# Half of a feed-forward up projection by Strassen's block products, on one core of a Trainium2 chip

## The chip, the cores and the metric

The kernel runs on one core of one Trainium2 chip. The metric is the device time of one execution in microseconds, compared by its median over several runs. The engines are named as in the profile: PE (TensorE, the matmuls), PEld (its weight loads), DVE (VectorE), ACT (ScalarE), POOL (GpSimd) and SP (SyncE, which here only issues transfers). Each works through its own list of instructions in order and waits for the others through semaphores.

## The reference

One layer of an encoder and a final norm, for a group of 512 tokens and one of 256 that share the weights; the kernel treats them as T = 768 columns. Cut to what matters:

```python
h = modulate(rmsnorm(x, norm1_g[l]), sh1, sc1)
proj = h @ w_in[l]          # attention, long convolution, gates
...
x = x + g1[:, None, :] * (merged @ w_out[l])
h = modulate(rmsnorm(x, norm2_g[l]), sh2, sc2)
x = x + g2[:, None, :] * (jnp.square(jax.nn.relu(h @ w_up[l])) @ w_down[l])
shf, scf = jnp.split(c_act @ w_ada_final + b_ada_final, 2, axis=-1)
return modulate(rmsnorm(x, final_g), shf, scf)
```

The width is 1024, the inner width 4096. `w_up` is 1024 x 4096, `w_down` 4096 x 1024. `sh1` to `g2` come from a product of a vector per group with `w_ada`.

## The kernel before

Activations lie transposed: channels on the 128 partitions, tokens along a row. A weight tile is 128 output channels by 1024 input channels, eight blocks of 128 x 128. To come near the precision of float32 with faster matmuls, every operand is split into a high part (rounded) and a low part (what is left): ACT makes the high part with a copy, DVE the low part by subtracting. A product is then three passes: high x high, high weight x low activation, low weight x high activation. The 768 tokens go through in two halves of 384 (`HALF`), so a tile is 8 blocks x 3 passes x 2 halves = 48 matmuls of 384 columns (`gemm_k`, L565).

The feed-forward part runs over four chunks of 1024 inner channels (`NCH`, loops in registers, written `Fori`). In `up(c)` PE makes eight tiles of hidden channels out of `act`; ACT takes the relu out of PSUM (L1288), DVE squares it (L1784), ACT copies the high part (L1291), DVE makes the low part (L1787). In `down(c)` PE multiplies the chunk with eight tiles of `w_down`, and DVE adds each result, times the gate, to `xT` (`residual`, L1724, three pieces). Both write into two slots of `acc_ps`, two banks each, in turn; PE may begin a tile when the reader of the one two before it is done (`acc_free`). SP loads raw tiles of 512 KB into two buffers `w_raw`, each when both parts of the tile before in it are made (`hi_done`, `lo_done`).

Two things are laid beside it. DVE computes the last 24 columns of the conditioning product ("late dots", L1771 and L1774: two reductions over 1024 elements and a small addition each) out of a ring that POOL loads: eight each in `up(0)`, `down(0)` and `down(1)`. And the last down projection is done for the 512 tokens of one group first and then for the 256 of the other (`PART_ORDER`, `group_k`, L643), so that the final norm of the first runs beside the second: residual (L1732), the sum of squares (ACT L1034, DVE L1348 and L1351), a sum over partitions on PE (L628, `norm_sum`), root and reciprocal (`norm_rstd`, L1356), a spread over the partitions on PE (L636), and the output. The scale of the final norm (`norm_scale`, L1362) is computed ahead of the last up projection. The first pair of up tiles is also done by halves (`side_k`, L650), one bank at a time.

The order of the work on each engine is the order in which the code is written; there is no scheduler. What lets an instruction start are the semaphores. The four banks `wk` of PSUM are unused in this part, but for the norms.

## Time and profile before

| | before |
|---|---|
| median of 3 runs | 1191.38 us (1187.12, 1191.38, 1192.0) |
| the profiled execution, its own time | 1186.96 us |
| its span | 1185.3 us |
| PE busy | 1152.7 us, 6618 matmuls |
| PEld busy | 1072.9 us |
| DVE busy | 682.6 us, 1136 instructions |
| ACT busy | 363.4 us, 551 instructions |
| POOL busy | 76.2 us |
| granted clock of PE, mean | 0.997 |

The span is the time from the first to the last instruction of the execution that the profiler recorded; its own time is some 1.7 us longer. Busy time is the sum of what an engine executed; matmuls overlap, so that for PE the distance from one start to the next says more than the length of one. The chain that ended last follows, back from the end, who released whom; an engine that holds a large share of it sets the time. The feed-forward part begins at about 640 us and ends with the kernel.

### The profile page before, as it was taken

What the parts mean: (1) busy time and instruction counts of PE and PEld (TensorE: products, weight loads), DVE (VectorE), ACT (ScalarE), POOL (GpSimd) and SP (SyncE); (2) the same over time, 40 slices, a digit from 0 to 9 for tenths busy, and PEclk for the clock granted to TensorE, in tenths of its full rate; (3) what the DMA queues carried; (4) which work ended last, traced back from release to release, by engine and by line L of the source; (5) the groups of instructions that cost most, each with busy time, mean ns of one, the idle gap of its engine ahead of it and who ended that gap; (6) DMA issues with size and microseconds to landing.
All of it is one profiled execution on the core that took longest, in us unless ns stands there. A gap on an engine that the chain in (4) does not pass through costs nothing.

```text
span 1185.3 us, 17412 instructions
## 1 busy us (share of the span) xinstructions
PE 1152.7 (97%) x6618; PEld 1072.9 (91%) x6618; DVE 682.6 (58%) x1136; ACT 363.4 (31%) x551; POOL 76.2 (6%) x110
## 2 busy tenths in 40 slices
PE   6899999999999999999999999999999999999997
PEld 3676678889899999999889999999999999999886
DVE  6767798878455754655546776643555343233434
ACT  5621135545611211412326331122211331122314
POOL 3001110000111110000000000000000000000000
PEclk9999999999999999999999999999999999999998
DMA  9915462231342322374213343322242121212202
GB/s 350 379 54 178 160 229 100 78 102 38 117 141 98 129 99 95 107 276 140 93 50 108 123 137 130 124 89 71 73 140 82 60 71 53 71 54 71 75 32 107
DMA packets 42849, 138.69 MB, mean 117 GB/s; under 512 B 4603, under 2 KB 10315, under 8 KB 41772
## 3 DMA queue, kind: packets, MB, share of 16 engines
q1 hardware_dynamic: 26544, 81.36, 20.2%
q0 software_dynamic: 11200, 43.78, 10.7%
q10 hardware_dynamic: 5052, 12.81, 3.2%
q8 instruction: 36, 0.59, 0.2%
q14 instruction: 17, 0.14, 0.0%
HBM read 122.20 MB, written 15.74 MB: 116 GB/s over the span
## 4 chain that ended last, share of the span: by engine, by line
PE 92%; DVE 5%; issue 1%; ACT 1%; DMA 1%; SPq 0%; DVEq 0%; ACTq 0%
PE acc_ps L565 66%; PE acc_ps L643 11%; PE wk L864 3%; PE wk L690 2%; PE wk L842 2%; PE wk L783 1%; PE wk L804 1%; DMA xT_in<-in_x_T 1%; PE wk L793 1%; PE wk L683 1%; PE acc_ps L650 1%; PE wk L756 0%; PE wk L817 0%; DVE hy_cross L1619 0%; DVE dot_out L1418 0%
## 5 line engine op out<-in xcount | busy, mean ns | idle before, releaser
L565 PE MATMUL acc_ps<-act_hilo,w_hi 128*128 128x384 f32 x2304 | 503.5, 339 | 5.1 <-DVE act_hilo L1373 3.6
L565 PEld LDWEIGHTS acc_ps<-act_hilo,w_hi 128*128 128x128 f32 x2304 | 405.1, 188 | 24.9 <-issue 22.0
L565 PE MATMUL acc_ps<-act_hilo,w_lo 128*128 128x384 f32 x1152 | 292.6, 334 | 0.0
L1327 DVE TENSOR_TENSOR w_lo<-w_raw,w_hi 128x1024 fp32r<-128x1024 f32 x102 | 124.5, 1221 | 174.9 <-ACT w_hi L1016 173.1
L565 PEld LDWEIGHTS acc_ps<-act_hilo,w_lo 128*128 128x128 f32 x1152 | 208.1, 188 | 0.0
L1016 ACT ACTIVATE w_hi<-w_raw 128x1024 fp32r<-128x1024 f32 x102 | 107.8, 1057 | 287.0 <-PE acc_ps L565 283.3
L565 PE MATMUL acc_ps<-hidden_hilo,w_hi 128*128 128x384 f32 x768 | 164.0, 334 | 0.0
L565 PEld LDWEIGHTS acc_ps<-hidden_hilo,w_hi 128*128 128x128 f32 x768 | 135.9, 188 | 0.0
L565 PE MATMUL acc_ps<-hidden_hilo,w_lo 128*128 128x384 f32 x384 | 97.5, 334 | 0.0
L1724 DVE SCALAR_TENSOR_TENSOR xT<-acc_ps,modT,xT 128x384 f32 (+2 forms) x72 | 30.4, 478 | 89.9 <-PE acc_ps L565 89.3
L565 PEld LDWEIGHTS acc_ps<-hidden_hilo,w_lo 128*128 128x128 f32 x384 | 69.3, 188 | 0.0
L1418 DVE CUSTOM_DVE_ANT_0 dot_out<-dot_ring,c_rows,vecT 128x1024 f32<-128x1024 f32 x48 | 61.5, 1281 | 0.9
L1771 DVE CUSTOM_DVE_ANT_0 dot_out<-dot_ring,c_rows 128x1024 f32<-128x1024 f32 x48 | 58.7, 1223 | 3.0 <-DVE hidden_hilo L1787 2.1
L1732 DVE SCALAR_TENSOR_TENSOR xT<-acc_ps,modT,xT 128x512 f32<-128x512 f32 (+1 forms) x32 | 19.7, 617 | 61.4 <-PE acc_ps L643 61.3
L1787 DVE TENSOR_TENSOR hidden_hilo<-n_h,hidden_hilo 128x768 f32 x32 | 30.7, 958 | 38.1 <-ACT hidden_hilo L1291 38.1
L643 PE MATMUL acc_ps<-hidden_hilo,w_down_hilo 128*128 128x512 f32 (+1 forms) x288 | 50.2, 336 | 0.0
L643 PEld LDWEIGHTS acc_ps<-hidden_hilo,w_down_hilo 128*128 128x128 f32 x288 | 44.4, 190 | 5.6
L1225 ACT ACTIVATE gates_out<-acc_ps 128x768 f32<-128x768 f32 x16 | 13.0, 812 | 117.2 <-PE acc_ps L565 117.2
L1291 ACT ACTIVATE hidden_hilo<-n_h 128x768 f32 x32 | 27.1, 847 | 64.4 <-DVE n_h L1784 64.4
L1648 DVE SCALAR_TENSOR_TENSOR hy_y<-hy_xv,vecT,hy_y 128x512 f32<-128x512 f32 (+1 forms) x16 | 17.2, 1124 | 35.0 <-POOL hy_y L537 35.0
L1583 DVE CUSTOM_DVE_ANT_0 att_s<-wk,mask,sink 128x256 f32<-128x256 f32 (+1 forms) x48 | 22.5, 524 | 22.1 <-PE wk L783 22.1
L643 PE MATMUL acc_ps<-hidden_hilo,w_hi 128*128 128x256 f32 (+1 forms) x128 | 32.0, 340 | 0.8 <-DVE hidden_hilo L1787 0.8
(212 smaller groups left out, 1279.8 us busy)
## 6 DMA issues: line engine op xcount, KB each, us to landing
w_raw<-in_w_pre SPq DMA_DIRECT2D x50, 512.0 KB, 3.3
dot_ring<-in_w_ada_cols POOLq DMA_DIRECT2D x48, 512.0 KB, 3.7
w_raw<-in_w_up SPq DMA_DIRECT2D x32, 512.0 KB, 3.3
w_raw<-in_w_down SPq DMA_DIRECT2D x32, 512.0 KB, 3.3
spec<-filt_out POOLq DMA_DIRECT2D x12, 512.0 KB, 3.1
gate_spill<-gates_out ACTq DMA_DIRECT2D x16, 384.0 KB, 2.3
hy_spec<-spec SPq DMA_DIRECT2D x12, 512.0 KB, 5.6
gates_in<-gate_spill ACTq DMA_DIRECT2D x16, 384.0 KB, 4.0
```

The costliest lines, as they stand in the source:

```text
L565: mm = pe.matmul(acc_ps[:, slot, 512 * h:512 * h + HALF], w[:, kw, :], src[:, x, k, HALF * h:HALF * h + HALF], start=(first and i == 0), s ...
L643: mm = pe.matmul(acc_ps[:, slot, half(h)], w_i[:, k, :], src[:, x, k, half(h)], start=(k == 0 and i == 0), stop=(k == KD - 1 and i == 2))
L690: mm = pe.matmul(wk[:, c + 512 * odd:c + 512 * odd + 512], tab[:, 2 * p + odd, j, P * q:P * q + P], taps[:, p, (2 * r if g else 0) + odd * ...
L842: mm = pe.matmul(o, w, v, start=(i == 0), stop=(i == len(terms) - 1))
L864: mm = pe.matmul(o, w, x, start=(i == 0), stop=(i == len(terms) - 1))
L1016: act_e.activation(whi[s][:] if to is None else to[0], raw[s][:], ACT.Copy).then_inc(hi_done, 1)
L1291: act_e.activation(hid[:, 0, bass.ds(i * 2 + s, 1), :].rearrange("p o n -> p (o n)"), hfB[:, s, :], ACT.Copy).then_inc(hid_hi, 1)
L1327: dve.tensor_tensor(lo, raw[s][:], hi, ALU.subtract).then_inc(lo_done, 1)
L1418: dve.tensor_tensor_reduce(junk[:], ring[:, i], cb[:, g], 1.0, vT[:, V_BA + mt:V_BA + mt + 1], ALU.mult, ALU.add, modT[:, mt, g:g + 1]).th ...
L1724: last = dve.scalar_tensor_tensor(row, acc_piece(s, a, b), modT[:, bass.ds(gate + m, 1), g:g + 1].rearrange("p o n -> p (o n)"), row, ALU. ...
L1771: dve.tensor_tensor_reduce(junk2[:], ring2[:, s], cb2[:, g], 1.0, 0.0, ALU.mult, ALU.add, dacc[:, g:g + 1]).then_inc(dot_done, 1)
L1787: dve.tensor_tensor(hid[:, 1, m, :].rearrange("p o n -> p (o n)"), hfB[:, s, :], hid[:, 0, m, :].rearrange("p o n -> p (o n)"), ALU.subtra ...
```

## The change

Two chunks stay as they were (`NCH` = 2), one done first and one last. Between them the other 2048 inner channels are done in four groups (`NHC`), each of two pairs of up tiles, `q` = 2 hc and 2 hc + 1, and then eight down tiles over the group's 512 inner channels.

A pair of up tiles is a 2 x 2 block product: two tiles of outputs, two halves of the input channels (`PK` = 4 blocks of 128), two halves of the tokens. Strassen's scheme (Winograd's variant) makes it out of seven products of sums of blocks. The sums of the activations (`t1` to `t4`) are made once, beside the first down projection. For each pair DVE makes four sums of weight blocks (`op_sum`), ACT and DVE split seven operands (`op_high`, `op_low`), PE computes the seven products into the four banks `wk` in turn (`product`, 12 matmuls of 384 columns each), ACT copies the first out (`first_copy`) and DVE puts the others together in seven additions (`combine_st`). Relu, square and copy of the four blocks are then ACT's (`hidden`), the low parts DVE's (`hidden_low`). The late dots of the down projections move into the second up projection and the last down projection, and `norm_scale(2)` moves behind the ninth residual of the last down projection. The diff, cut to its core:

```diff
@@ -34,7 +34,12 @@
 HW = 512
 GATE0 = HY0 + 3 * HW
 DFF = 4 * D
-NCH = DFF // D
+NCH = 2
+NHC = 4
+PK = KD // 2
+ST_READ = (0, 1, 2, 3, 5, 6, 7)
+ST_DOWN = (4, 6, 5)
+ST_ORDER = ((0, 1, 2, 3, 5, 4, 6), (0, 1, 2, 3, 4, 5, 6), (0, 2, 1, 3, 5, 4, 6))
...
+        def st_ps(q, j):
+            c = 512 * ((7 * q + j) % 4)
+            return wk[:, c:c + HALF]
+
+        def op_count(r, j):
+
+            return 7 * r + ST_ORDER[min(r, 1 + (r + 1) % 2)].index(j) + 1
+
...
+            def pair_used(q, side):
+
+                n = max(op_count(q, j) for j in ((0, 2), (5,))[side])
+                sp.wait_ge(op_hi, n)
+                sp.wait_ge(op_lo, n)
+                sp.wait_ge(st_sum, 4 * q + 4)
+
...
+            for hc in range(NHC):
+                for side in range(2):
+                    pair_used(2 * hc, side)
+                    sp.dma_start(raw[side][:], w_up[2 * KD + 4 * hc + 2 + side]).then_inc(ld_sa[side], 16)
+                for m in range(KD):
+                    if m < 4:
+                        pair_used(2 * hc + 1, m // 2)
+                    else:
+                        tiles_used(KD * hc + m - 3)
+                    sp.dma_start(quarter(m % 4), w_half[KD * hc + m]).then_inc(ld_sd[m % 4], 16)
+                for side in range(2):
+                    tiles_used(KD * hc + 6 + 2 * side)
+                    if hc < NHC - 1:
+                        sp.dma_start(raw[side][:], w_up[2 * KD + 4 * hc + 4 + side]).then_inc(ld_sa[side], 16)
+                    else:
+                        sp.dma_start(raw[side][:], w_up[KD + side]).then_inc(landed[side], 16)
+            up_weights(1, first=1)
+            down_weights(1)
             for m in range(KD):
...
+            def product(q, j):
+
+                hi, lo = st_weight(j)
+                pe.wait_ge(op_hi, op_count(q, j))
+                pe.wait_ge(op_lo, op_count(q, j))
+                if (q, j) == (0, 1):
+                    pe.wait_ge(t_hi, 4)
+                    pe.wait_ge(t_lo, 4)
+                q4, j4 = divmod(7 * q + j - 4, 7)
+                if q4 >= 0 and j4 == 0:
+                    pe.wait_ge(st_p1, q4 + 1)
+                elif q4 >= 0:
+                    pe.wait_ge(st_u, 7 * q4 + ST_READ[j4])
+                for k in range(PK):
+                    for i, (w, x) in enumerate(((hi, 0), (hi, 1), (lo, 0))):
+                        mm = pe.matmul(st_ps(q, j), w[:, k, :], st_act(j, x, k),
+                                       start=(k == 0 and i == 0), stop=(k == PK - 1 and i == 2))
+                mm.then_inc(st_mm, 1)
+
+            def st_down(hc, m):
+
+                s = m % 2
+                hi, lo = st_weight(ST_DOWN[m % 3])
+                pe.wait_ge(sd_hi, KD * hc + m + 1)
+                pe.wait_ge(sd_lo, KD * hc + m + 1)
+                if hc == 0 and m < 2:
+                    pe.wait_ge(acc_free[s], A_MLP // 2 + KD)
+                else:
+                    pe.wait_ge(sd_free, KD * hc + m - 1)
+                for n, k in enumerate((0, 1, 3, 2)):
+                    if m == 0 and k != 1:
+                        need = 8 * hc + {0: 4, 3: 7, 2: 8}[k]
+                        pe.wait_ge(h4_hi, need)
+                        pe.wait_ge(h4_lo, need)
+                    for i, (w, x) in enumerate(((hi, 0), (hi, 1), (lo, 0))):
+                        for h in range(2):
+                            mm = pe.matmul(acc_ps[:, s, 512 * h:512 * h + HALF], w[:, k, :], hid4[:, x, k, HALF * h:HALF * h + HALF],
+                                           start=(n == 0 and i == 0), stop=(n == PK - 1 and i == 2))
+                mm.then_inc(sd_ready, 1)
+
             up(0, first=1)
             down(0)
-            with pe.Fori(1, NCH - 1) as c:
-                up(c)
-                down(c)
+            for hc in range(NHC):
+                for q in (2 * hc, 2 * hc + 1):
+                    for j in range(7):
+                        product(q, j)
+                for m in range(KD):
+                    st_down(hc, m)
+            pe.wait_ge(sd_free, KD * NHC)
             up(NCH - 1)
             for u, (h, m) in enumerate(PART_ORDER):
...
+            def op_high(r, j):
+
+                if j in (0, 2):
+                    act_e.wait_ge(ld_sa[0], 16 * (r + 2))
+                elif j == 5:
+                    act_e.wait_ge(ld_sa[1], 16 * (r + 2))
+                else:
+                    act_e.wait_ge(st_sum, 4 * r + {4: 1, 1: 2, 3: 3, 6: 4}[j])
+                if r == 0:
+                    act_e.wait_ge(acc_ready, A_MLP + (15 if j < 2 else 16))
+                elif r % 2 or j < 4:
+                    act_e.wait_ge(st_mm, 7 * (r - 1) + j + 1)
+                else:
+                    act_e.wait_ge(sd_ready, KD * (r // 2 - 1) + {4: 7, 5: 6, 6: 8}[j])
+                act_e.activation(st_weight(j)[0], st_source(j), ACT.Copy).then_inc(op_hi, 1)
+
...
+            def first_copy(q):
+
+                act_e.wait_ge(st_mm, 7 * q + 1)
+                if q:
+                    act_e.wait_ge(h4_lo, 4 * (q - 1) + 3)
+                act_e.activation(c_block(2), st_ps(q, 0), ACT.Copy).then_inc(st_p1, 1)
+
+            def hidden(q, b):
+
+                n = 4 * q + b + 1
+                act_e.wait_ge(st_u, 7 * q + (2, 4, 6, 7)[b])
+                act_e.activation(c_block(b), c_block(b), ACT.Relu).then_inc(st_relu, 1)
+                act_e.wait_ge(st_relu, 2 * n - 1)
+                act_e.activation(c_block(b), c_block(b), ACT.Square).then_inc(st_relu, 1)
+                act_e.wait_ge(st_relu, 2 * n)
+                act_e.activation(hid_block(q, b, 0), c_block(b), ACT.Copy).then_inc(h4_hi, 1)
...
+            def op_low(r, j):
+
+                dve.wait_ge(op_hi, op_count(r, j))
+                hi, lo = st_weight(j)
+                dve.tensor_tensor(lo, st_source(j), hi, ALU.subtract).then_inc(op_lo, 1)
+
+            def down_low(hc, m):
+
+                dve.wait_ge(sd_hi, KD * hc + m + 1)
+                hi, lo = st_weight(ST_DOWN[m % 3])
+                dve.tensor_tensor(lo, quarter(m % 4), hi, ALU.subtract).then_inc(sd_lo, 1)
+
+            def combine_st(q, n):
+
+                j = (1, 2, 3, 4, 4, 5, 6)[n]
+                dve.wait_ge(st_mm, 7 * q + j + 1)
+                if n < 2:
+                    dve.wait_ge(st_p1, q + 1)
+                else:
+                    dve.wait_ge(st_u, 7 * q + (0, 0, 2, 3, 1, 4, 5)[n])
+                if q and n in (0, 1, 3):
+                    dve.wait_ge(h4_lo, 4 * (q - 1) + {0: 4, 1: 1, 3: 2}[n])
+                dst, other = (c_block(b) for b in ((3, 2), (0, 2), (2, 3), (1, 2), (3, 3), (2, 2), (3, 3))[n])
+                dve.tensor_tensor(dst, st_ps(q, j), other, ALU.add).then_inc(st_u, 1)
+
+            def hidden_low(q, b):
+
+                dve.wait_ge(h4_hi, 4 * q + b + 1)
+                dve.tensor_tensor(hid_block(q, b, 1), c_block(b), hid_block(q, b, 0), ALU.subtract).then_inc(h4_lo, 1)
+
+            def st_residual(hc, m):
+
+                s = m % 2
+                dve.wait_ge(sd_ready, KD * hc + m + 1)
+                if hc == 0:
+                    dve.wait_ge(acc_free[s], A_MLP // 2 + KD)
+                else:
+                    dve.wait_ge(sd_free, KD * (hc - 1) + m + 1)
+                for g, a, b in PIECES:
+                    last = dve.scalar_tensor_tensor(xT[:, m, a:b], acc_piece(s, a, b), modT[:, G2 + m, g:g + 1],
+                                                    xT[:, m, a:b], ALU.mult, ALU.add)
+                last.then_inc(sd_free, 1)
+
...
+            for hc in range(NHC):
+                q = 2 * hc
+                combine_st(q, 0)
...
+                else:
+                    op_sum(q + 1, 0)
+                    op_sum(q + 1, 1)
+                    op_low(q + 1, 0)
+                    op_low(q + 1, 1)
+                    combine_st(q, 1)
+                    op_sum(q + 1, 2)
+                    op_sum(q + 1, 3)
+                    combine_st(q, 2)
+                    hidden_low(q, 0)
+                    op_low(q + 1, 2)
+                    combine_st(q, 3)
+                    combine_st(q, 4)
+                    op_low(q + 1, 3)
+                combine_st(q, 5)
+                hidden_low(q, 1)
+                if hc == 0:
+                    op_low(1, 3)
+                op_low(q + 1, 4)
+                combine_st(q, 6)
+                hidden_low(q, 2)
+                op_low(q + 1, 5)
+                q = 2 * hc + 1
+                hidden_low(q - 1, 3)
+                op_low(q, 6)
+                combine_st(q, 0)
+                combine_st(q, 1)
+                combine_st(q, 2)
+                hidden_low(q, 0)
+                combine_st(q, 3)
+                combine_st(q, 4)
+                down_low(hc, 0)
+                combine_st(q, 5)
+                hidden_low(q, 1)
+                combine_st(q, 6)
+                hidden_low(q, 2)
+                down_low(hc, 1)
+                hidden_low(q, 3)
+                down_low(hc, 2)
+                for m in range(KD):
+                    if m == KD - 1 and hc < NHC - 1:
+                        op_sum(q + 1, 3)
+                        op_low(q + 1, 3)
+                        op_low(q + 1, 5)
+                    st_residual(hc, m)
+                    if m + 3 < KD:
+                        down_low(hc, m + 3)
+                    if m >= KD - 2 and hc == NHC - 1:
+                        split_w(T_MLP + 16 + m % 2, m % 2, 16 * (landed_base + 9))
+                    if m == 5 and hc < NHC - 1:
+                        op_low(q + 1, 0)
+                        op_low(q + 1, 2)
+                    if m == 6 and hc < NHC - 1:
+                        op_sum(q + 1, 0)
+                        op_sum(q + 1, 1)
+                        op_sum(q + 1, 2)
+                        op_low(q + 1, 1)
+                    if m == KD - 1 and hc < NHC - 1:
+                        op_low(q + 1, 4)
+                        op_low(q + 1, 6)
+            dve.wait_ge(ld_c, 48)
+            up(NCH - 1, dots=KD)
             for u, (h, m) in enumerate(PART_ORDER):
                 dve.wait_ge(acc_ready, A_MLP + 16 * (NCH - 1) + KD + u + 1)
-                dve.wait_ge(acc_free[u % 2], A_MLP // 2 - 3 + KD * (NCH - 1) + m // 2)
+                if not h:
+                    dve.wait_ge(sd_free, KD * (NHC - 1) + m + 1)
                 residual_group(u % 2, m, G2, h)
                 if u < KD - 2:
                     t = T_MLP + 16 * (NCH - 1) + KD + u + 2
                     split_w(t, u % 2, 16 * (landed_base + (t - T_MLP) // 2 + 1), to=w_last(u + 2))
                 if u <= KD or u == 2 * KD - 1:
                     acc_half(2, u, h)
+                if u < KD:
+                    late_dot(2 * KD, u // 2, u % 2)
                 if u == KD:
+                    dve.wait_ge(late_done, DOTS - DOTS_OUT + 1)
+                    norm_scale(2)
                     norm_rstd(2, 0)
```

In the odd pairs of a group no weights of a next pair are prepared; those of the group behind are prepared beside its down tiles. How the change stands on the engines, at three places.

DVE, one up tile before (the low part of a weight tile, the square, the low part of the hidden tile, registers and a wait between them):

```order
L1327 TENSOR_TENSOR w_lo1<-w_raw1,w_hi1 128x1024
L1784 TENSOR_TENSOR n_h<-ev_tmp 128x768
L1785 REGISTER_ALU
L1787 ISA
L1787 REGISTER_ALU
L1787 TENSOR_TENSOR hidden_hilo<-n_h,hidden_hilo 128x768
```

DVE, the beginning of an even pair after the change (`c_st` are the blocks being put together, `s1_sum` to `s4_sum` sums of weight blocks of the odd pair behind it, `w_lo0`, `w_lo1` low parts):

```order
L2100 TENSOR_TENSOR c_st<-wk,c_st 128x384
L2075 TENSOR_TENSOR s1_sum<-w_raw1 128x512
L2075 TENSOR_TENSOR s2_sum<-s1_sum,w_raw0 128x512
L2081 TENSOR_TENSOR w_lo0<-w_raw0,w_hi0 128x512
L2081 TENSOR_TENSOR w_lo0<-s2_sum,w_hi0 128x512
L2100 TENSOR_TENSOR c_st<-wk,c_st 128x384
L2075 TENSOR_TENSOR s3_sum<-w_raw0,w_raw1 128x512
L2075 TENSOR_TENSOR s4_sum<-w_raw0,s2_sum 128x512
L2100 TENSOR_TENSOR c_st<-wk,c_st 128x384
L2105 TENSOR_TENSOR hid_st<-c_st,hid_st 128x384
L2081 TENSOR_TENSOR w_lo1<-w_raw0,w_hi1 128x512
L2100 TENSOR_TENSOR c_st<-wk,c_st 128x384 x2
```

Where DVE had a low part, a square and a low part of 768 or 1024 elements for each tile, it now has additions out of PSUM with the sums and low parts of the next pair between them.

ACT, the end of an odd pair after the change (L1486 relu, L1488 square, L1490 high part of a hidden block; L1473 high part of a down tile of the same group):

```order
L1486 ACTIVATE c_st<-c_st 128x384
L1488 ACTIVATE c_st<-c_st 128x384
L1490 ACTIVATE hid_st<-c_st 128x384
L1473 ACTIVATE w_st_hilo<-w_raw0 128x512
L1486 ACTIVATE c_st<-c_st 128x384
L1488 ACTIVATE c_st<-c_st 128x384
L1490 ACTIVATE hid_st<-c_st 128x384
L1473 ACTIVATE w_st_hilo<-w_raw1 128x512 x2
```

The last hidden block of the group stands behind the high part of the second down tile.

DVE, the end of the first group of tokens in the last down projection, before and after (its last two residuals and what follows, L1732 and L1992 are the residual):

```order
L1732 SCALAR_TENSOR_TENSOR xT<-acc_ps,modT,xT 128x512
L1351 TENSOR_TENSOR n_acc<-n_acc,n_t 128x512
L1732 SCALAR_TENSOR_TENSOR xT<-acc_ps,modT,xT 128x256
L1348 COPY n_acc<-n_sq 128x256
L1356 RECIPROCAL norm_rstd<-norm_rstd 128x4
```

```order
L1992 SCALAR_TENSOR_TENSOR xT<-acc_ps,modT,xT 128x512
L1611 TENSOR_TENSOR n_acc<-n_acc,n_t 128x512
L2031 ISA dot_out2,dot_sum<-dot_ring2,c_rows2 128x1024
L2031 ISA dot_sum 128x1
L2031 ISA dot_out2,dot_sum<-dot_ring2,c_rows2 128x1024
L2031 ISA dot_sum 128x1
L2034 TENSOR_SCALAR modT<-dot_sum,vecT 128x2
L1992 SCALAR_TENSOR_TENSOR xT<-acc_ps,modT,xT 128x256
L1608 COPY n_acc<-n_sq 128x256
L1622 SCALAR_TENSOR_TENSOR norm_scale<-modT,vecT 128x8 x2
L1616 RECIPROCAL norm_rstd<-norm_rstd 128x4
```

A late dot stands between the eighth residual's accumulation and the ninth residual, and the norm scales stand ahead of the reciprocal.

## Rows read from the trace of the kernel before

**Rows 1.** The page: busy time by engine, and the chain that ended last
```profile
PE 1152.7 (97%) x6618; PEld 1072.9 (91%) x6618; DVE 682.6 (58%) x1136; ACT 363.4 (31%) x551; POOL 76.2 (6%) x110
...
PE 92%; DVE 5%; issue 1%; ACT 1%; DMA 1%; SPq 0%; DVEq 0%; ACTq 0%
```

**Rows 2.** The chain in order of time: start us, us, what
```profile
484.00 83.20 PE acc_ps L565 x480
...
655.16 449.58 PE acc_ps L565 x2592
```

**Rows 3.** Timeline, first up tiles: start us, us, engine line op tiles
```profile
652.64 0.51 PE L650 MATMUL acc_ps<-act_hilo,w_hi 128*128 128x384 f32 x2
```

**Rows 4.** Waits from 600 us on: total us, times, longest us
```profile
DVE hidden_hilo L1787 <- ACT hidden_hilo L1291: 38.1, 32, 1.2
...
PE acc_ps L643 <- DVE hidden_hilo L1787: 0.8, 1, 0.8
```

**Rows 5.** Groups by form, DVE and ACT: busy us, mean ns, idle before
```profile
L1327 DVE TENSOR_TENSOR w_lo<-w_raw,w_hi 128x1024 fp32r<-128x1024 f32 x58 | 70.8, 1220 | 104.8 <-ACT w_hi L1016 104.0 <-issue 0.8
...
L1388 DVE TENSOR_TENSOR act_hilo<-n_h,act_hilo 128x512 fp32r<-128x512 f32 x8 | 5.5, 684 | 1.2 <-ACT act_hilo L1067 1.2
...
L1388 DVE TENSOR_TENSOR act_hilo<-n_h,act_hilo 128x256 fp32r<-128x256 f32 x8 | 3.4, 425 | 2.4 <-ACT act_hilo L1067 2.4
...
L1067 ACT ACTIVATE act_hilo<-n_h 128x512 fp32r<-128x512 f32 x8 | 5.1, 632 | 0.3
...
L1067 ACT ACTIVATE act_hilo<-n_h 128x256 fp32r<-128x256 f32 x8 | 3.3, 418 | 0.3
```

**Rows 6.** Timeline, first matmul of a down tile, ACT, a residual
```profile
705.21 0.85 PE L565 MATMUL acc_ps<-hidden_hilo,w_hi 128*128 128x384 f32 x4
...
705.49 1.06 ACT L1016 ACTIVATE w_hi<-w_raw 128x1024 fp32r<-128x1024 f32 x1 [3.31 <-PE acc_ps L565]
...
714.50 1.27 DVE L1724 SCALAR_TENSOR_TENSOR xT<-acc_ps,modT,xT 128x384 f32 x3 [0.53 <-DVE modT L1774]
```

**Rows 7.** Timeline, DVE: one dot
```profile
716.82 1.22 DVE L1771 CUSTOM_DVE_ANT_0 dot_out<-dot_ring,c_rows 128x1024 f32<-128x1024 f32 x1
...
717.96 0.08 DVE L1771 DVE_READ_ACCUMULATOR2_ANT dot_sum<- 128x1 f32 x1
...
719.58 0.23 DVE L1774 TENSOR_SCALAR modT<-dot_sum,vecT 128x2 f32 x1 [0.27 <-DVE dot_sum L1771]
```

**Rows 8.** Timeline of the last down projection, DVE and PE
```profile
1109.27 0.96 DVE L1787 TENSOR_TENSOR hidden_hilo<-n_h,hidden_hilo 128x768 f32 x1 [1.23 <-ACT hidden_hilo L1291]
...
1110.38 0.70 PE L643 MATMUL acc_ps<-hidden_hilo,w_hi 128*128 128x512 f32 x2 [0.84 <-DVE hidden_hilo L1787]
...
1111.35 0.75 DVE L1732 SCALAR_TENSOR_TENSOR xT<-acc_ps,modT,xT 128x512 f32<-128x512 f32 x1 [1.12 <-PE acc_ps L643]
...
1116.82 0.75 DVE L1732 SCALAR_TENSOR_TENSOR xT<-acc_ps,modT,xT 128x512 f32<-128x512 f32 x1 [3.25 <-PE acc_ps L643]
...
1118.62 0.69 DVE L1351 TENSOR_TENSOR n_acc<-n_acc,n_t 128x512 f32<-128x512 f32 x1
...
1150.90 0.69 DVE L1351 TENSOR_TENSOR n_acc<-n_acc,n_t 128x512 f32<-128x512 f32 x1 [0.70 <-ACT n_t L1034]
...
1151.77 0.95 PE L628 MATMUL wk<-ones,n_acc 128*128 128x1 f32 x8
...
1153.22 0.48 DVE L1732 SCALAR_TENSOR_TENSOR xT<-acc_ps,modT,xT 128x256 f32<-128x256 f32 x1 [1.63 <-PE acc_ps L643]
...
1154.40 0.17 DVE L1356 RECIPROCAL norm_rstd<-norm_rstd 128x4 f32<-128x4 f32 x1
...
1154.62 1.16 PE L636 MATMUL wk<-ident,norm_rstd 128*128 128x128 f32 x8 [0.73 <-DVE norm_rstd L1356]
```

**Rows 9.** Norm scale by form (1038 to 1106 us); a weight load, us to landing
```profile
L1362 DVE SCALAR_TENSOR_TENSOR norm_scale<-modT,vecT 128x8 f32<-128x8 f32 x2 | 0.2, 160 | 0.0
...
w_raw<-in_w_up SPq DMA_DIRECT2D x32, 512.0 KB, 3.3
```

More of the change, by code:

```diff
@@ new lines, in t_high @@
+            def t_high(n, src, dst):
+                act_e.wait_ge(t_step, n)
+                act_e.activation(dst, src[:], ACT.Copy).then_inc(t_hi, 1)
+            up(0)
+            for u in range(KD):
+                if u < KD - 2:
+                    split_w(T_MLP + KD + 2 + u, u % 2, 16 * (landed_base + 6 + u // 2))
+                if u == 1:
+                    t_high(3, t_f1, t1[:, 0])
+                if u == 2:
+                    t_high(5, t_f2, t2[:, 0])
+                if u == 5:
+                    t_high(10, t_f2, t3[:, 0])
+                    act_e.wait_ge(t_lo, 3)
+                    t_high(10, t_f1, t4_hi[:])
@@ L1943, in laid_out @@
     h["w_up"] = tiles(np.asarray(inputs["w_up"])[0])
[L1944 to L1945 removed]
+    down = np.asarray(inputs["w_down"])[0]
+    h["w_down"] = np.concatenate([tiles(down[D * i:D * i + D]) for i in range(NCH)])
+    h["w_down_half"] = np.concatenate([tiles(w) for w in down[D * NCH:].reshape(NHC, PK * P, D)])
     return {n: np.ascontiguousarray(v) for n, v in h.items()}
```

249 lines of the change are left out of this document (211 added, 38 removed).

## The prediction

> **What bounds the kernel.** I read the page first: TensorE (PE) is busy for 97% of the span, and 92% of the chain that ended last is PE [rows 1]. The reader should see that ACT and DVE can only matter where PE waits for them. Then the chain in order of time: the feed-forward part is one piece, 2592 matmuls of 384 columns in 449.58 us, so 173.4 ns from start to start [rows 2]. Straight-line code does the same: 480 in 83.20 us, 173.3 ns. So neither the loops nor their absence cost PE anything. In the list of waits PE waits only once from there on before the end of the last down projection, 0.8 us for the last hidden tiles [rows 4]. Whatever removes matmuls there removes time, as long as PE stays fed.
>
> **What it removes.** A pair of up tiles took 2 tiles x 8 k x 3 passes x 2 token halves = 96 matmuls; seven products of 4 k x 3 passes are 84. Eight pairs: 96 matmuls fewer. The new ones write one bank in a row instead of two in turn. The first up tiles already do that: two in 0.51 us with 334 ns for one, so the second starts some 0.17 us after the first [rows 3]. Hence 96 x 173.4 ns = **16.6 us gained**. The down half keeps its number: 4 x 8 tiles x 4 k x 3 x 2 = 768 matmuls, as before. Weight bytes do not change.
>
> **What it adds on DVE and ACT.** Prices, from the lengths of like instructions [rows 5]: on DVE 1024 elements take 1220 ns, 512 take 684, 256 take 425; so 384 take 0.555 us and 1536 (the activation sums) about 1.76. On ACT 512 take 632, 256 take 418, so 384 take 0.525. Neighbours overlap by about 0.08 us (the next DVE instruction after 716.82 + 1.22 started at 717.96). PE's end is seen 0.28 us after the next tile's first matmul started (705.21 to 705.49) [rows 6]; DVE's end is seen by PE after 0.14 us (1109.27 + 0.96 to 1110.38) [rows 8].
> - *The seven sums of the activations*, with their splits (ten sums, four highs, four lows), stand in the first down projection, where each tile gives DVE 8.3 us (48 x 173.4 ns). The fullest tile, the seventh, has a residual of 1.27 us [rows 6], two lows of 1536 and four 512-long ones: 1.27 + 3.4 + 2.5 = 7.2 us. It fits with about 1 us left; price nothing. Without that cover the first product would wait by the excess.
> - *An even pair* (its products take 84 x 0.1734 = 14.6 us) also carries the split of the odd pair behind it: 11 instructions of 512 and 11 of 384 on DVE, 11 x 0.684 + 11 x 0.555 = 13.6 us, less 21 overlaps of 0.08 = 11.9 us. It starts late: in the last two tiles of the down before it, seven 512-long instructions stand between the seventh residual and the eighth, which ends 2.9 us after that tile's matmuls (-4.16 + 0.28 + 1.27 + 7 x 0.604 + 1.27); two lows follow, to 4.1. The first combine can start at 4.4 (two products of 2.08, 0.28 until seen). Combine and four 512-long: 7.3, the second combine; it and two sums: 9.1, the third; then the first hidden low waits for ACT (7.9 + three steps of 0.545 = 9.5), itself and a 512-long low bring 10.8, the fourth, and 11.3, the fifth; from there PE sets the pace, 12.8 and 14.9. The bank of the second product is wanted back at 10.4 (by the sixth), those of the third to fifth at 12.5, 14.6 and 16.6: four and a half microseconds are spare, and about four for the weights of the fifth to seventh product. The raw pairs take 3.3 us to land [rows 9] and are asked for about when the even pair starts; the first sum wants them at 4.9. Price nothing.
> - *An odd pair* has half that work. Here one wait is real. The down tile that follows takes its inner blocks in the order 0, 1, 3, 2; block 2 is read after 18 matmuls, at 3.12 us, and needs the hidden block made from the last product. That is: 0.28 until seen, combine 0.555, but ACT is still in the high part of a down tile until 1.05; relu, square and copy, each waiting for the one before, 3 x 0.545 = 1.63, to 2.7; the low part 0.555, to 3.25; 0.14 to PE, 3.4. PE waits **0.3 us, four times: 1.2 us**. No row shows such a chain; from below it is 0 (ACT 0.3 us earlier each time), from above 1.0 each, 4 us, if the three ACT steps and the two hand-offs cost a third more. I take 1.2, next to the rows.
> - *PE waits for the last residual* before the second up projection (a wait on all 32 residuals, where there were two buffers): 0.28 + 1.27 + 0.14 = **1.7 us**, once. Queued behind are the whole up projection's matmuls. Nothing hides it.
> - *The dots that were in the down projections* move: eight to the second up, eight to the last down. In the up they cost nothing (the first up carries the same eight without holding PE up). In the last down a tile of 512 columns lasts 5.44 us (5.47 for the first, 1111.35 to 1116.82). One dot is two reductions and an addition, 716.82 to 719.81, 2.91 us to the next instruction [rows 7]. Walk: hidden low ends at 1110.23, then comes the last up dot: DVE is free at 1113.4 where the first residual stood at 1111.35, 2.1 us late. A tile then needs 1.80 + 0.61 + 2.91 = 5.32 us (the accumulation starts 1.80 us after its residual, 1118.62 after 1116.82), so the lag shrinks 0.12 us a tile to 1.4 at the seventh tile; without a split the period is 4.97, the eighth residual is 0.9 us late. PE's sum for the norm at 1151.77 needs the accumulation of 1150.90 + 0.69 + 0.9 = 1152.5: **0.7 us**. Behind it stands the eighth dot, DVE is free at 1155.3, and the ninth residual (1153.22) is 2.1 us late; then the two norm scales, moved here, 2 x 160 ns less overlaps [rows 9]. The reciprocal of 1154.40 comes at 1156.75, PE's spread of 1154.62 at 1156.97: **2.35 us in all**, the 0.7 included. Bounds: 0 if DVE caught up by then, 5.4 (a tile) if each dot took half a microsecond longer.
>
> **Sum.** 16.6 - 1.2 - 1.7 - 2.35 = 11.4 us off the profiled execution: its own 1186.96 us becomes 1175.6 (the span 1185.3 becomes 1173.9). The three runs before it were 1187.12, 1191.38 and 1192.0; on their median the same gain gives **1180.0 us**, -0.96%.
>
> **A rule that speaks against it.** The fixed part of a DVE instruction here is what is left at zero length of 1220 and 684 ns: 0.15 us, half of it overlapped. The Trainium skill, page "VectorE: DVE Perf Modes", in its section on the TRN2 errata, says that VectorE and ScalarE pay a latency between instructions and advises tiles of at least 512 elements, so that it carries less weight; the change goes the other way, with 384-long pieces. By the page's formula of (N + 151)/0.96 ns, an estimate, 384 elements take 0.557 us, where the rows give 0.555; the sum stays. It feeds the chance of the next rival, nothing else.
>
> **Rivals.**
> 1. *DVE becomes the bound in the even pairs: slower than before.* It happens if the hand-offs from ACT are exposed: seven lows wait for their highs, four hidden lows for ACT's copy. Before, such a wait is 38.1 us / 32 = 1.19 us [rows 4]. All eleven exposed: 11.9 + 13.1 = 25 us, where a pair's 14.6 and the 4.5 spare allow 19.1; PE loses 5.9 us in each of four even pairs: 24 - 11.4 = 12 us slower, 1204. PE starts to wait at a DVE stretch of 19.1 us (0.65 us a hand-off), and the kernel is slower than before above 22 (0.9). For it: DVE's load is 82% of PE's, the waits exist. Against: in the order written, other DVE work stands between nearly every high and its low, and ACT has its own slack (about 11 us in 14.6).
> 2. *Small stalls eat half.* The chain behind the last product costs 1.0 instead of 0.3 (+2.8), the last down loses a whole tile (+3): gain 5.6, 1185.8. For it: three margins in the walk are under 1 us (block 2, the seventh tile of the first down, the lag in the last down). Against: each length comes from a row.
> 3. *Everything is hidden but the 1.7 us:* gain 14.9, 1176.5. It needs ACT 0.3 us earlier four times, and a DVE that catches up 2.1 us in seven tiles; the dots alone speak against it.
>
> **Chances.** Forecast 0.66; rival 1 0.07 in full, and 0.04 at the threshold of no change; rival 2 0.13; rival 3 0.10. About 0.5%, 6 us, is what a measurement of this kernel can tell. Forecast and rival 3 are faster, and a third of rival 2: 0.80. Same 0.13, slower 0.07. The range: 1173 (rival 3 on a run like the lowest, 1187.12) to 1187 (rival 2 with a run like the highest).
>
> **What would show it.** The products: 672 matmuls of 384 columns into wk, 173 ns apart, none with a wait; 2.08 us a product. In the list of waits: PE for hid_st four times, near 0.3 us; PE for the last residual once, 1.7; PE's norm sum and spread together 2.35 above before. DVE about 12 busy us per even pair. A granted clock of 1.00 through it, as now. I am wrong if PE waits in the middle of a pair, for a low part or for a bank, if the products stand further apart than 173 ns, or if the last down tiles show DVE without idle time and PE waiting for weights.

## The result and the profile after

| | changed kernel | kernel before |
|---|---|---|
| median, us (runs) | 1177.72 (4) | 1191.69 (4) |
| lowest to highest, us | 1177.17 to 1180.96 | 1187.12 to 1192.14 |
| ratio of the times | 0.9888, 95% interval 0.9867 to 0.9908 | |

The changed kernel is 1.1% faster; the forecast was 1180.0 us. The execution that was profiled is its longest, 1180.96 us, with a span of 1179.3.

The page of the changed kernel, against [rows 1]: 96 matmuls fewer, 9 us less of PE, 206 instructions and 96 us more on DVE. That PE's busy time falls by 9 us, and not by the 16.6 us of the matmuls that went, is the lower clock of this execution, 0.990 against 0.997: in *tail* and *best* below, at 0.997, it falls by 16.5 and 17.1. In the row PEclk the second place, 29 to 59 us, is now 8, ahead of the part that was changed. What the clock does behind PE's waits is too short for slices of 29 us and is shown below.

```profile
PE 1143.8 (97%) x6522; PEld 1061.9 (90%) x6522; DVE 778.9 (66%) x1342; ACT 413.6 (35%) x683; POOL 76.9 (7%) x111
...
PEclk9899999999999999999999999999999999999998
```

Its chain in order of time (start us, us, what), the counterpart of [rows 2]. L1103 is a product, 168 matmuls being an even and an odd pair; L1124 is a down projection of half the inner channels.

```profile
658.90 116.75 PE acc_ps L677 x672
775.65 29.12 PE wk L1103 x168
804.77 33.41 PE acc_ps L1124 x192
838.18 29.12 PE wk L1103 x168
867.30 33.43 PE acc_ps L1124 x192
...
992.38 33.46 PE acc_ps L1124 x192
...
1027.56 68.45 PE acc_ps L677 x384
...
1101.66 39.04 PE acc_ps L755 x171
...
1147.00 1.16 PE wk L748 x8
1148.16 20.94 PE acc_ps L755 x162
```

What to see: each pair of pairs takes 29.12 us, and the next entry starts at once. 29.12 / 168 is 173.3 ns, so no product waits. The 384 matmuls of the last up loop take 68.45 us where 384 x 173.3 is 66.57, and the last 162 take 20.94 where before they took 19.45 (same view of the kernel before, from 1155.78). The feed-forward part, from the first entry above to the end of the span, is 1179.3 - 658.90 = 520.4 us; before it is 1185.3 - 655.16 = 530.1 [rows 2]. So 9.7 us came out of the part that was changed.

PE's waits in this part (total us, times, longest us), the counterpart of [rows 4]:

```profile
PE wk L748 <- DVE norm_rstd L1616: 2.4, 2, 1.8
PE acc_ps L677 <- DVE xT L2116: 1.7, 1, 1.7
PE wk L740 <- DVE n_acc L1611: 1.5, 1, 1.5
PE acc_ps L755 <- DVE hidden_hilo L2047: 0.9, 1, 0.9
```

The third and fourth stand in the kernel before as well (1.5 and 0.8). The second is new. The first was 0.7 at its longest [rows 8].

Behind both long waits the granted clock falls. Stretches of 2 us (columns: us, then busy time of each engine, PEclk, DMA share, GB/s), first behind the wait for the last residual, then behind the wait for the norm:

```profile
1026.00:1028.00 2.00, 0.44 (x2) 0.44 (x3) 2.00 (x4) 0.00 (x0) 0.00 (x0) 1.00 0.60 246
1028.00:1030.00 2.00, 2.00 (x10) 2.00 (x10) 0.26 (x1) 0.00 (x0) 0.00 (x0) 0.69 0.34 35
1030.00:1032.00 2.00, 2.00 (x8) 2.00 (x7) 0.00 (x0) 0.00 (x0) 0.00 (x0) 0.50 0.61 227
1032.00:1034.00 2.00, 2.00 (x13) 2.00 (x12) 0.00 (x0) 0.00 (x0) 0.00 (x0) 0.95 0.00 0
...
1147.00:1149.00 2.00, 2.00 (x14) 2.00 (x15) 0.69 (x1) 0.02 (x1) 0.00 (x0) 0.81 0.00 0
1149.00:1151.00 2.00, 2.00 (x12) 2.00 (x11) 0.00 (x0) 0.79 (x1) 0.00 (x0) 0.50 0.16 60
```

PE is busy for the whole of a stretch and does only 8 matmuls in it, instead of 13: 0.50 is 1.2 GHz. The loop behind the wait of 1.7 us thus took 1.9 us more than its matmuls. Of these 1.6 are the clock's: where it holds, as in *again* below, the loop still takes 66.85 us, 0.3 more than 66.57. A busy column does not show this; the count in it and PEclk do.

DVE in the even pair that starts at 838.18 (timeline: start us, us, ...), for which the prediction had a walk:

```profile
842.38 0.56 DVE L2100 TENSOR_TENSOR c_st<-wk,c_st 128x384 f32<-128x384 f32 x1
844.97 0.69 DVE L2075 TENSOR_TENSOR s_sum<-w_raw 128x512 f32<-128x512 f32 x1 [2.04 <-DMA w_raw<-in_w_up]
...
847.75 0.55 DVE L2100 TENSOR_TENSOR c_st<-wk,c_st 128x384 f32<-128x384 f32 x1
...
851.09 1.02 DVE L2100 TENSOR_TENSOR c_st<-wk,c_st 128x384 f32<-128x384 f32 x2
```

The first, second and fourth combine start 4.2, 9.6 and 12.9 us into the pair; the walk had 4.4, 7.3 and 10.8. DVE stood for 2.04 us because the raw pair had landed only at 6.8, and not before 4.9: SP issued its two loads only from 838.78 to 840.29. PE did not notice.

The last down projection, DVE and PE (timeline), the counterpart of [rows 8]:

```profile
1104.72 0.75 DVE L1992 SCALAR_TENSOR_TENSOR xT<-acc_ps,modT,xT 128x512 f32<-128x512 f32 x1
...
1106.85 1.22 DVE L2031 CUSTOM_DVE_ANT_0 dot_out<-dot_ring,c_rows 128x1024 f32<-128x1024 f32 x1
...
1109.52 0.75 DVE L1992 SCALAR_TENSOR_TENSOR xT<-acc_ps,modT,xT 128x512 f32<-128x512 f32 x1
...
1114.58 0.74 DVE L1992 SCALAR_TENSOR_TENSOR xT<-acc_ps,modT,xT 128x512 f32<-128x512 f32 x1
...
1140.72 0.75 DVE L1992 SCALAR_TENSOR_TENSOR xT<-acc_ps,modT,xT 128x512 f32<-128x512 f32 x1 [0.62 <-PE acc_ps L755]
...
1143.04 0.95 PE L740 MATMUL wk<-ones,n_acc 128*128 128x1 f32 x8
...
1145.45 0.48 DVE L1992 SCALAR_TENSOR_TENSOR xT<-acc_ps,modT,xT 128x256 f32<-128x256 f32 x1
```

Count from the start of the down, 1101.66 here and 1110.38 before. The first residual stands at 3.06 instead of 0.97, which is 2.1 late. A late tile lasts 5.06 us on DVE (1109.52 to 1114.58) and 5.44 on PE, so the lag is gone before the eighth: its residual is at 39.06, before 39.08, and waits for PE. The norm sum is at 41.38, before 41.39. Only the last dot still stands ahead of the ninth residual: 43.79 instead of 42.84, and the spread is at 45.34 instead of 44.24, 1.1 late.

### The profile page after: what moved, and what is told of

The parts are those of the page before. It is cut to its first block, busy times and chain, and to the rows that moved or that the text cites. A ratio compares the mean times of both kernels' runs of the same rounds, so it can differ in the third digit from the quotient of the medians.

```text
span 1179.3 us, 17099 instructions
## 1 busy us (share of the span) xinstructions
PE 1143.8 (97%) x6522; PEld 1061.9 (90%) x6522; DVE 778.9 (66%) x1342; ACT 413.6 (35%) x683; POOL 76.9 (7%) x111
## 4 chain that ended last, share of the span: by engine, by line
PE 92%; DVE 4%; issue 1%; ACT 1%; DMA 1%; SPq 0%; DVEq 0%; ACTq 0%
PE acc_ps L677 44%; PE acc_ps L1124 11%; PE acc_ps L755 11%; PE wk L1103 10%; PE wk L976 3%; PE wk L802 2%; PE wk L954 2%; PE acc_ps L762 1%; PE wk L895 1%; PE wk L916 1%; PE wk L905 1%; PE wk L795 1%; DMA xT_in<-in_x_T 1%; PE wk L868 0%; PE wk L929 0%
## 5 line engine op out<-in xcount | busy, mean ns | idle before, releaser
L677 PE MATMUL acc_ps<-act_hilo,w_hi 128*128 128x384 f32 x1792 | 398.1, 343 | 6.1 <-DVE act_hilo L1633 3.0
L677 PEld LDWEIGHTS acc_ps<-act_hilo,w_hi 128*128 128x128 f32 x1792 | 317.8, 190 | 26.6 <-issue 23.5
L677 PE MATMUL acc_ps<-act_hilo,w_lo 128*128 128x384 f32 x896 | 229.2, 336 | 0.0
L677 PEld LDWEIGHTS acc_ps<-act_hilo,w_lo 128*128 128x128 f32 x896 | 163.5, 190 | 0.0
L1587 DVE TENSOR_TENSOR w_lo<-w_raw,w_hi 128x1024 fp32r<-128x1024 f32 x70 | 85.5, 1222 | 91.9 <-ACT w_hi L1172 90.9
L1124 PE MATMUL acc_ps<-hid_st,w_st_hilo 128*128 128x384 f32 x768 | 134.3, 335 | 0.0
L1124 PEld LDWEIGHTS acc_ps<-hid_st,w_st_hilo 128*128 128x128 f32 x768 | 133.0, 188 | 0.7 <-issue 0.7
L2116 DVE SCALAR_TENSOR_TENSOR xT<-acc_ps,modT,xT 128x384 f32<-128x384 f32 (+2 forms) x96 | 40.6, 479 | 58.9 <-PE acc_ps L1124 58.9
L677 PE MATMUL acc_ps<-hidden_hilo,w_hi 128*128 128x384 f32 x256 | 54.7, 334 | 0.0
L1992 DVE SCALAR_TENSOR_TENSOR xT<-acc_ps,modT,xT 128x512 f32<-128x512 f32 (+1 forms) x32 | 19.7, 616 | 39.7 <-PE acc_ps L755 39.5
L677 PEld LDWEIGHTS acc_ps<-hidden_hilo,w_hi 128*128 128x128 f32 x256 | 45.3, 188 | 0.0
L1473 ACT ACTIVATE w_st_hilo<-w_raw 128x512 fp32r<-128x512 f32 x32 | 20.2, 630 | 69.5 <-PE acc_ps L1124 62.9
```

Of the source, the lines that this page charges most:

```text
L677: mm = pe.matmul(acc_ps[:, slot, 512 * h:512 * h + HALF], w[:, kw, :], src[:, x, k, HALF * h:HALF * h + HALF], start=(first and i == 0), s ...
L1124: mm = pe.matmul(acc_ps[:, s, 512 * h:512 * h + HALF], w[:, k, :], hid4[:, x, k, HALF * h:HALF * h + HALF], start=(n == 0 and i == 0), sto ...
L1587: dve.tensor_tensor(lo, raw[s][:], hi, ALU.subtract).then_inc(lo_done, 1)
L2116: last = dve.scalar_tensor_tensor(xT[:, m, a:b], acc_piece(s, a, b), modT[:, G2 + m, g:g + 1], xT[:, m, a:b], ALU.mult, ALU.add)
```

## Experiments

My theory after this result: the matmuls removed are worth their full 16.6 us; against them stand the wait for the last residual (1.7 us and some 1.9 by the clock), the late dots (1.1 and some 1.5 by the clock) and almost nothing else. The rivals are those of the prediction, above all a DVE that is about to be the bound. The numbers below are medians, and the feed-forward part of the profiled execution (from the first matmul of its first up loop to the end of the span), since the kernel's first 60 us vary by themselves (last section). The first four kernels were timed beside each other in 5 rounds (kernel before: 1191.62 us, 11 runs), the other four in 3 rounds on another chip (1190.64, 13 runs).

**The changed kernel again** (*again*), no edit.

> The changed kernel itself, beside its variants on the same chip. Theory: all its matmuls' gain is there, 16.6 us, and it gives back 6.7: PE waits 1.7 us for the last residual and 1.8 us at the norm's spread (0.7 before), and after each of these the granted clock stands at half for about 3.4 us, which costs 1.9 and 1.5 us. From the first tile of the up loop to the end I expect 520.4 us (530.1 in the kernel before); over the runs 11 to 14 us less than before. Rival: the 13 us between the medians is mostly the start of the program and the feed-forward part gives less than 8.

Measured: 1179.68 us, ratio 0.9905 (0.9883 to 0.9928); part 520.0 us. The waits are the same, 1.7 and 1.8. The clock is not. Behind the 1.7 us wait it holds, and the last up loop takes 66.85 instead of 68.45 us. Behind the 1.8 us wait it falls earlier than in the first trace, and eight matmuls of the spread take 2.07 us instead of 1.16. Stretches of this run:

```profile
1028.00:1030.00 2.00, 2.00 (x14) 2.00 (x13) 0.00 (x0) 0.00 (x0) 0.00 (x0) 1.00 0.65 150
...
1144.00:1150.00 6.00, 5.41 (x25) 5.41 (x26) 1.22 (x5) 0.94 (x2) 0.00 (x0) 0.50 0.12 44
```

So the same wait of the same kernel is followed by a fall in one execution and not in another.

**The wait for the residuals, one slot at a time** (*slot*)**.** The second up projection starts when 31 of the 32 residuals are done, and its second tile waits for the last.

```diff
-            pe.wait_ge(sd_free, KD * NHC)
-            up(NCH - 1)
+            pe.wait_ge(sd_free, KD * NHC - 1)
+            up(NCH - 1, last=KD * NHC)
...
+                        if last is not None and s == 1:
+                            pe.wait_ge(sd_free, last)
```

> PE waits before the second up projection only for the residual of the slot that it writes: the first tile for the seventh residual of the last group, the second for the eighth. Theory (the wait brings the fall of the clock): the wait of 1.7 us goes and the 1.9 us at half clock with it, 3.6 us less than the changed kernel; clock 1.00 from 1020 to 1040 us. Rival (the fall has another cause, such as the new mix of work): 1.7 us less and still some 3.4 us at half clock near that place.

Measured: 1174.54 us, ratio 0.9857 (0.9833 to 0.988); part 515.6 us, 4.3 less than the changed kernel beside it. In its chain the loop follows the down at once and runs at full clock:

```profile
993.83 33.41 PE acc_ps L1126 x192
1027.23 66.57 PE acc_ps L677 x384
...
1145.93 19.45 PE acc_ps L755 x162
```

The 1.7 us is gone from the list of waits. Of the 4.3, 1.7 is the wait and 0.3 the loop. The clock behind the spread gives 2.8, since it held here though its wait of 1.8 us is still there, and 0.5 is lost again in the last 10 us. These two are not the edit's doing. As the clock did not fall behind the 1.7 us wait in *again* either, this pair of traces does not settle whether the wait brings the fall; *group* does.

**The late dots one place earlier** (*tail*)**.** Each dot of the last down moves a tile forward, the first of them to the head of the second up projection; none stands ahead of the ninth residual any more (the two buffers that the rows for the dots are loaded into change places with them).

```diff
+            late_dot(KD, 0, 0)
-            up(NCH - 1, dots=KD)
+            up(NCH - 1, dots=KD + 1)
...
-                if u < KD:
-                    late_dot(2 * KD, u // 2, u % 2)
+                if u < KD - 1:
+                    late_dot(2 * KD + 1, u // 2, u % 2)
```

> The sixteen moved late dots come one place earlier: one ahead of the second up projection, eight in it, seven in the last down projection, none between the eighth and the ninth residual. Theory: the ninth residual is no longer behind a dot; PE waits about 0.7 us at its norm sum and 0.7 to 0.8 at the spread, each too short for the clock to fall: 0.4 us of waits and 1.5 us of half clock less, 1.9 in all. Rival (the clock falls after any wait there, or PE's total idle counts): 0.4 us less, clock still 0.5 near 1150 us.

Measured: 1177.34 us, ratio 0.9888 (0.9864 to 0.9912), 2.3 below the changed kernel beside it, which the scatter of the medians covers; part 516.2 us, 3.7 less. The waits say it more clearly: the longest for the norm is 0.9 instead of 1.8, and the last 162 matmuls take 19.45 us.

```profile
PE wk L748 <- DVE norm_rstd L1616: 1.4, 2, 0.9
```

Of the 3.7, 2.8 is the clock, which held behind the spread. That the shorter wait is why it held is not shown: in *slot*, *eight* and *group* it held behind 1.8 us too. Here the 1.7 us wait was again without a fall of the clock (66.85 us for the loop).

**Both, and the last hidden block ahead of the second down tile's weights** (*best*)**.** On ACT and on DVE the step for the last hidden block goes one place forward, so that a wait for it in the down projection would go.

```diff
-                down_high(hc, 1)
                 hidden(q, 3)
+                down_high(hc, 1)
...
-                down_low(hc, 1)
                 hidden_low(q, 3)
+                down_low(hc, 1)
```

> Both of these, and the last hidden block of each group ahead of the second down tile on ACT and DVE. Theory: 3.6 + 1.9 + 0.5 = 6.0 us less than the changed kernel, 1.6% less than before; no half clock but in the last 10 us. Rival (no clock effect): 1.7 + 0.4 + 0.5 = 2.6 us less.

Measured: 1170.75 us, ratio 0.9838 (0.9813 to 0.9864), the fastest of all, 1.6% below the kernel before and 8.9 us below the changed one. The part is 514.3 us, 5.7 less. Of the 5.7, 2.8 is once more the clock behind the spread in *again*; the waits that are gone or shorter give the rest. The other 3.2 are the part ahead of it: three of its four runs had a mean clock of 0.997, the six of the changed kernel 0.988 to 0.994. The down projections:

```profile
800.39 33.41 PE acc_ps L1126 x192
...
1021.39 66.57 PE acc_ps L677 x384
```

192 x 173.3 is 33.28, so 0.13 us stay in each (the three not shown are 33.43, 33.41 and 33.41). The edit did not bring the block earlier. Timelines of the first of these down projections in the changed kernel and then here (first matmul, the last low part of a hidden block, the weight load behind the first 18):

```profile
804.61 3.58 PE L1124 MATMUL acc_ps<-hid_st,w_st_hilo 128*128 128x384 f32 x19
807.07 0.56 DVE L2105 TENSOR_TENSOR hid_st<-c_st,hid_st 128x384 fp32r<-128x384 f32 x1 [0.64 <-ACT hid_st L1490]
807.75 0.30 PEld L1124 LDWEIGHTS acc_ps<-hid_st,w_st_hilo 128*128 128x128 f32 x2 [0.17 <-issue]
...
800.23 3.58 PE L1126 MATMUL acc_ps<-hid_st,w_st_hilo 128*128 128x384 f32 x19
802.69 0.56 DVE L2108 TENSOR_TENSOR hid_st<-c_st,hid_st 128x384 fp32r<-128x384 f32 x1 [1.24 <-ACT hid_st L1492]
803.36 0.30 PEld L1126 LDWEIGHTS acc_ps<-hid_st,w_st_hilo 128*128 128x128 f32 x2 [0.17 <-issue]
```

In both the low part ends 3.02 us into the down projection, and PE loads the 19th weights 0.12 or 0.11 us after it, having stood for 0.17. ACT's relu for this block starts 0.79 us in, in both, so the high part of the down tile that stood ahead of it had not held it up. This is the wait that the prediction derived, at the place that it named, only shorter.

**Eight for seven** (*eight*)**.** The seventh product is computed twice: 12 matmuls more in each pair, 96 in all, and nothing else.

```diff
-                for k in range(PK):
+                for k in [k for _ in range(2 if j == 6 else 1) for k in range(PK)]:
```

> The seventh product of each pair is computed twice in a row (its first twelve matmuls are overwritten), so a pair has 96 matmuls again and everything else stays. Theory (the gain is the matmuls taken out, and PE is the bound in every pair): 8 x 12 x 173.3 ns = 16.6 us more than the changed kernel, from the first tile of the up loop to the end 536.6 to 537 us; a pair of products 16.64 us where it is 14.56. Rival (part of the gain is hidden because PE would wait for DVE or ACT in the pairs anyway): less than 12 us more, with waits of PE gone.

Measured: 1197.23 us, ratio 1.0063 (1.0041 to 1.0084), 17.5 above the changed kernel's 1179.68; part 535.4 us, 1.2 below what was expected, since the clock held behind the spread (19.45 us for the last 162 matmuls), though it fell behind the last residual (68.43 for the loop). Its chain gives the price without scatter:

```profile
773.09 33.28 PE wk L1103 x192
```

33.28 - 29.12 = 4.16 us for 24 matmuls, 16.64 for the four groups. The removed product is worth the whole of its matmul time. Without it the changed kernel is slower than the one before by what the reordering costs.

**PE waits for the last residual ahead of groups 2 to 4** (*group*)**.**

```diff
             for hc in range(NHC):
+                if hc:
+                    pe.wait_ge(sd_free, KD * hc)
```

> PE also waits, ahead of the products of groups 2 to 4, for the last residual of the group before, which DVE ends 2.9 us after the last down matmul (it stands behind seven instructions for the next pair). Theory (a wait costs itself and may bring the clock down behind it): three waits of 3.0 us, 9.0 us; and behind each the clock at half for up to 3.4 us, up to 1.7 us each, 5 more: 9 to 14 us more in that part, and a clock of 0.5 in windows behind the waits. Rival (no effect on the clock from waits of this length): 9.0 us and clock 1.00.

Measured: 1193.34 us (10 runs), ratio 1.0018 (1.0003 to 1.0033), 13.7 above the changed kernel; part 532.7 us (from 659.80), 12.7 more. The waits add up to 8.9 us:

```profile
PE wk L1103 <- DVE xT L2118: 8.9, 3, 3.0
```

They are 3.0 each, not 1.7, since other DVE work stands between the last two residuals there, as in the prediction's walk. Behind all three the clock falls; the third:

```profile
976.00:978.00 2.00, 1.21 (x4) 1.21 (x5) 1.94 (x5) 0.00 (x0) 0.00 (x0) 0.50 0.89 322
...
980.00:982.00 2.00, 2.00 (x8) 2.00 (x7) 0.00 (x0) 0.96 (x2) 0.00 (x0) 0.50 0.00 0
```

The 168 products of that group take 32.07 us instead of 29.12, 2.95 more. The 0.3 that stands behind a wait at full clock is in it, so some 2.7 are the clock's. At these three places the clock of the changed kernel is 1.00, and nothing but PE's waits was added: this is the run that shows that a wait brings the fall. Three waits of PE between the groups eat the whole gain.

**More work for DVE in the even pairs** (*lows1*, *lows2*)**.** The rival that DVE is nearly the bound: each of the seven low parts that it makes for the odd pair is computed twice (once more), then three times (twice more). One costs 0.7 us with its wait, so 5 and 10 us in each even pair.

```diff
                 hi, lo = st_weight(j)
+                for _ in range(1 if r % 2 else 0):
+                    steps[0] += 1
+                    dve.tensor_tensor(lo, st_source(j), hi, ALU.subtract).then_inc(f_step, 1)
+                    dve.wait_ge(f_step, steps[0])
```

> Each low part of an odd pair's operands is made twice, the second after the first has ended: seven instructions, 7 x 0.72 = 5.0 us more on DVE in each even pair. Theory (DVE has slack there, about 2.4 us at the tightest bank and more behind): PE waits under 0.5 us a pair, the kernel is at most 1 us longer. Rival (DVE is at its limit in the even pairs): 4 x 3 to 5 us, 12 to 20 us longer, slower than before.

Measured, once more: 1182.13 us, ratio 0.9931 (0.9905 to 0.9956), 2.5 to 4.4 above the changed kernel's two medians. PE waits 3.5 us in all for it:

```profile
PE acc_ps L1124 <- DVE hid_st L2109: 3.0, 5, 0.8
...
PE wk L1103 <- DVE c_st L2104: 0.5, 1, 0.5
```

The theory had at most 1, the rival 12 to 20. The part is 523.3 us (from 657.01), 3.3 more. The rival falls, but the slack is smaller than I had it: 5 us more are already felt at the hidden blocks.

> The same with each of these low parts made three times: 10 us more on DVE in each even pair. The bank of the third product, wanted at 12.5 us and read at 10.1 now, is read at 13.0; what follows gets later by up to 10 us, less some 3.5 us in which DVE waits now. Theory: PE waits 2 to 5 us in each even pair or at the start of the odd one, 8 to 20 us in all, and each wait may bring the clock down. Rival (the prediction's walk, 4.5 us spare and 19.1 us allowed for a stretch of 21.9): 2.8 us a pair, 11 us. Both are waits for combines, not for low parts.

Measured, twice more: 1205.8 us, ratio 1.0131 (1.0111 to 1.0152); part 544.9 us (from 659.30).

```profile
PE wk L1103 <- DVE c_st L2104: 14.2, 16, 2.7
PE acc_ps L1124 <- DVE hid_st L2109: 4.6, 8, 0.8
```

18.8 us of waits, within what was expected. So the mechanism of the rival is real: PE waits for a bank that a combine has yet to free, and the kernel ends on the slower side. The point from which it decides lies between 5 and 10 us more of DVE in an even pair.

## Why the prediction was right, step by step

1. *What it removes, 16.6 us.* Right to the digit: 29.12 us for 168, and 16.64 taken back by the eighth product. That the seven products write one bank in a row cost nothing.
2. *The seven sums in the first down projection, price nothing.* Right. 672 matmuls in 116.75 us are 0.3 above 672 x 173.3, as much as the 2592 of before were above theirs.
3. *An even pair, price nothing.* Right in the price, wrong in the walk. DVE was busy 12.6 us in the stretch 838 to 853, near the 11.9 that I had. But from the second combine on it was 2.1 to 2.3 us late, since I gave the raw pair 3.3 us to land from the start of the pair, and it landed at 6.8. That was half of the 4.5 us that I held to be spare, which fits with 5 us more for DVE being felt and 10 hurting.
4. *An odd pair, 0.3 us four times.* The down projections were 0.13 to 0.18 us above 192 x 173.3, 0.6 in all, not 1.2. The wait is at block 2, where I had it, and its size was wrong. I held ACT busy with the high part of a down tile until 1.05; it was done by 0.89, and the relu started at 0.79, right behind the combine. So the low part ended at 3.02 and not at 3.25, and PE gets there at 3.12: with the 0.14 of the hand-off it is late by hundredths, and 0.13 is the whole of what each down projection loses.
5. *The last residual, 1.7 us.* Measured 1.74, and gone when the wait was split by slots. What I priced was the wait alone; the loop behind it takes 0.3 more even at full clock (66.85 against 66.57).
6. *The last down projection, 2.35 us.* Measured 1.1. The step that failed is the length of a dot. I took 2.91 us from [rows 7], where its last addition had waited 0.27 us for the second reduction; in the last down the dots took 2.67 (1106.85 to 1109.52). A tile of DVE was then 5.06 us instead of 5.32, and the lag, which began at the 2.1 that I had, lost 0.38 a tile instead of 0.12. It was gone before the norm sum (0.7 expected, 0.0 measured), and only the eighth dot was left, with 0.95.
7. *"A granted clock of 1.00 through it, as now."* Wrong. In the profiled execution 1.9 us were lost behind the last residual, 1.6 of them by the clock and the 0.3 of step 5, and 1.5 by the clock behind the spread. The prediction had looked for what PE waits for, and put what a wait does to the clock at nothing.

The sum for this execution: -16.6 + 0.6 + 1.7 + 1.9 + 1.1 + 1.5 = -9.8 us, measured -9.7; predicted -11.4. The terms mis-sized (together 1.85 us too dear) and what was left out (3.4) partly cancel, so the time was nearer than the working deserves. That is luck, and so is some of the agreement of the medians. Between the medians it is -14.0 us in the first comparison and -11.9 in the second; the difference to the part is made ahead of it, where the code is the same in both kernels (last section).

Of the rivals, the first exists but is 5 to 10 us of DVE away from deciding. The second, small stalls, named the wrong stalls. The third, everything hidden but the 1.7 us, gave 14.9, and no kernel here is that one. *best*, which has lost the 1.7 us too, comes to 15.8 (a part of 514.3 against 530.1).

## What to carry to other kernels

Where the chain of waits is one piece of TensorE, count the matmuls that go: they are worth their full start-to-start time, if PE never stops between them. Then list each place where PE does stop, and price a stop by more than its length, since in some executions the clock halves behind it, which cost 1.5 to 2.8 us each time here. A wait on everything that a pool of buffers holds is better split, so that the first tile waits only for its own buffer; and work that can be late anywhere should not be the last thing ahead of the result that PE waits for.
